# Neighbourhood attention on one core: the scores of the two new row tiles moved to the head of each step of TensorE's queue

## What is computed

```python
def one_row(r):
    rs = clip(r - 4, 0, rows - 8)
    k_blk, v_blk = the rows rs .. rs+7, the columns near each query
    s = einsum(q_row, k_blk); s = where(mask, s + bias, -1e30)
    p = softmax(s, axis=(-2, -1))
    return einsum(p, v_blk)
```

## Time and profile before

| | |
|---|---|
| time of the runs | 2304.22 us median of 3 (2302.72 to 2304.95) |
| time of the profiled execution | 2304.31 us |
| its span | 2302.5 us, 32169 instructions |
| TensorE products busy | 2245.8 us, 98% |
| VectorE busy | 1227.9 us, 53% |
| ScalarE busy | 902.1 us, 39% |
| GpSimd busy | 1074.2 us, 47% |
| chain that ended last | 87% of it TensorE |

### The profile page before, as it was taken

One profiled execution on the slowest core, in us unless ns is written; L12 is line 12 of the kernel. 1 busy time (PEld: TensorE's weight loads), 2 busy tenths in 40 slices (PEclk: granted clock), 3 DMA queues, 4 the chain that ended last, 5 costly groups with the idle time before them and its releaser, 6 DMA issues.

```text
span 2302.5 us, 32169 instructions
## 1 busy us (share of the span) xinstructions
PE 2245.8 (98%) x11948; PEld 1840.5 (80%) x11948; DVE 1227.9 (53%) x2065; ACT 902.1 (39%) x1793; POOL 1074.2 (47%) x777
## 2 busy tenths in 40 slices
PE   7999999999999999999999999999999999999998
PEld 6788888888788888888879867767878888888886
DVE  4644444546654444577753255555575444347767
ACT  5531111256223333344654345554642333334443
POOL 4112222467988888400234322313789888780000
PEclk9999999999999999999999999999999999999999
DMA  5121111342343323553353434243523433338334
GB/s 215 46 83 46 47 46 46 129 167 108 115 132 138 110 96 110 214 213 95 107 178 102 138 91 103 68 129 120 193 81 131 159 103 108 103 103 327 97 96 156
DMA packets 138573, 279.11 MB, mean 121 GB/s; under 512 B 34531, under 2 KB 55602, under 8 KB 136370
## 3 DMA queue, kind: packets, MB, share of 16 engines
q1 hardware_dynamic: 138418, 277.05, 36.2%
HBM read 207.80 MB, written 69.23 MB: 120 GB/s over the span
## 4 chain that ended last, share of the span: by engine, by line
PE 87%; DVE 3%; POOL 2%; ACT 1%; issue 1%; DMA 1%; SPq 0%; DVEq 0%; POOLq 0%; ACTq 0%
PE PS L2114 26%; PE PS L2116 26%; PE PS L2115 26%; PE PS L2396 2%; PE PS L2583 2%; PE PS L2601 2%; PE PS L2504 1%; POOL wlo L827 1%; DVE SB L1851 1%; PE PS L2429 1%; PE PS L2492 1%; PE PS L2384 1%; POOL rstd L856 0%; PE PS L2517 0%; PE PS L2516 0%
## 5 line engine op out<-in xcount | busy, mean ns | idle before, releaser
L2114 PE MATMUL PS<-AOP,OPS 128*128 128x512 f32 x1216 | 474.3, 390 | 5.1 <-DVE AOP L1666 3.2
L2116 PE MATMUL PS<-AOP,OPS 128*128 128x512 f32 x1216 | 473.5, 389 | 0.0
L2115 PE MATMUL PS<-AOP,OPS 128*128 128x512 f32 x1216 | 473.4, 389 | 0.0
L827 POOL TENSOR_TENSOR wlo<-stage,whi 128x1024 fp32r<-128x1024 f32 (+1 forms) x88 | 207.8, 2366 | 407.5 <-ACT whi L1057 407.2
L880 POOL TENSOR_TENSOR OPS<-TW,OPS 128x512 fp32r<-128x512 f32 x176 | 260.8, 1497 | 77.3 <-ACT OPS L1143 77.3
L2114 PE MATMUL PS<-aT,whi 128*128 128x512 f32 (+1 forms) x672 | 273.7, 407 | 7.3 <-DVE bdK L1917 3.6
L2114 PEld LDWEIGHTS PS<-AOP,OPS 128*128 128x128 f32 x1216 | 228.3, 188 | 54.4 <-POOL OPS L880 4.0
L2116 PEld LDWEIGHTS PS<-AOP,OPS 128*128 128x128 f32 x1216 | 228.3, 188 | 47.5
L2115 PEld LDWEIGHTS PS<-AOP,OPS 128*128 128x128 f32 x1216 | 228.4, 188 | 47.1
L2116 PE MATMUL PS<-aT,wlo 128*128 128x512 f32 (+1 forms) x672 | 261.4, 389 | 0.0
L2115 PE MATMUL PS<-aT,whi 128*128 128x512 f32 (+1 forms) x672 | 260.5, 388 | 0.0
(11 more groups left out here) (213 smaller groups left out, 4062.4 us busy)
## 6 DMA issues: line engine op xcount, KB each, us to landing
stage<-in_w SPq DMA_DIRECT2D x100, 512.0 KB, 3.8
hidden_scratch<-HT SPq DMA_DIRECT2D x154, 256.0 KB, 2.2
SRAW<-hidden_scratch SPq DMA_DIRECT2D x154, 256.0 KB, 2.6
stage<-in_wpack SPq DMA_DIRECT2D x76, 512.0 KB, 3.3
BW<-in_w SPq DMA_DIRECT2D x16, 1024.0 KB, 8.0
h_scratch<-Hb SPq DMA_DIRECT2D x24, 512.0 KB, 3.2
Hb<-h_scratch SPq DMA_DIRECT2D x24, 512.0 KB, 6.0
cat_scratch<-OC SPq DMA_DIRECT2D x14, 512.0 KB, 3.0
```

The source lines that it names most:

```text
L827: pool.tensor_tensor(wlo[:, slot, cols], stage[:, slot, cols], whi[:, slot, cols].bitcast(F32), ALU.subtract)\
L2114: pe.matmul(dst, stat[0], mov[0], start=start, stop=False, skip_group_check=onto)
L2115: pe.matmul(dst, stat[0], mov[1], start=False, stop=False, skip_group_check=onto)
L2116: return pe.matmul(dst, stat[1], mov[0], start=False, stop=stop, skip_group_check=onto)
```

## The change

`pair_scores(T)` moves from behind `filler(T)` to the head of the step, ahead of `turn_probs` of tile T-3 and of `filler(T)`. No instruction is added or taken away, and no wait is altered. The other engines' queues stay as they are.

```diff
             tiles = HP * ROWS
             for T in range(0, tiles + 4, 2):
+                if T < tiles:
+                    pair_scores(T)
                 if 0 <= T - 3 < tiles:
                     turn_probs(R_ROW + T - 3)
                 filler(T)
-                if T < tiles:
-                    pair_scores(T)
                 if 0 <= T - 4 < tiles:
                     pair_values(T - 4)
                 if 0 <= T - 2 < tiles:
                     turn_probs(R_ROW + T - 2)
                 filler(T + 1)
```

## The result

The changed kernel takes 2314.11 us (median of six runs, 2312.63 to 2315.2) against 2304.14 us for the kernel before beside it (six runs, 2302.72 to 2304.95): ratio 1.0043, 95% interval 1.0032 to 1.0053, so 10 us slower. The profiled execution took 2313.19 us with a span of 2311.4 us, 8.9 more than before.

The account below looks back on a forecast made before the run. TensorE's own time bounds the loop's first 200 us; in the last 53 us the chain through VectorE and ScalarE counts too. 5.6-1.2+0.7+2.4 = +7.5 us on 2304.31 gives 2311.8 us, range 2305.0 to 2316.0.

Parts of the forecast that it names:

- Joints in dense steps: TensorE, steps 4 to 76: changed neighbours among products cost 0.15 us per step in 37 steps, +5.6 us.
- S-Tr in the 360-column form: Start of the last score product to the following transposes of probabilities: taken as 0.77 us, as scores to values.
- F-V: Projection piece followed by value products: 0.33 us against 0.23 for projection to transposes, +0.10 per step.
- Tr-F: Transposes followed by projection: 0.30 us behind scores against 0.24 behind projection, +0.05 rounded per step.
- Waits in the dense part: First 200 us of the loop: four transpose waits go, -1.2 us; scores of four steps wait 0.2 each, +0.7.
- Waits in the tail: Last 53 us of the loop: new waits of scores and values +6.3 us, old waits that vanish -5.1.
- Waits that go: Last 53 us of the loop: old waits of transposes, projection and scores vanish, -5.1 us in sum.
- five small waits: Loop's tail: new waits at four score pairs (tiles 80, 86, 92, 94) and the values of tile 77, together 1.2 us.
- the clock plays no part: Both loop stages: TensorE's clock is at its full level, so nothing was booked for it.
- That the joints cost nothing: Rival, TensorE's joints: their 6.8 us vanish and +0.7 of waits is left, 2305.0 us; chance 0.14.
- That the head frees the chain: Rival, whole loop: earlier peaks, exponentials and normalising shrink TensorE's waits by 5.3 us, 2299.0 us; chance 0.04.
- That the head waits in every dense step: Rival, dense part: late peaks hold the scores in each of 38 steps, 11.4 us on top, 2323.2 us; chance 0.08.

Follow-up runs that it names:

- Run 3: Kernel before, old order, with the projection piece of steps 0 to 76 cut in two around the scores: 2309.83 us, ratio 1.0019.
- Run 5: Changed kernel run again: 2312.87 us, ratio 1.0040; then with ScalarE's last weight split in the loop behind tile 90, not 89: 2311.14 us, ratio 1.0032.
- runs 1: Kernel before with scores moved to the step's head only in steps 0 to 76, old order from step 78: 2309.59 us, ratio 1.0019.
- run 8: Changed kernel with VectorE's three operand splits one place later and ScalarE's two weight splits moved to tiles 80 and 92: 2307.08 us, ratio 1.0010.
- run 6: Changed kernel with VectorE's operand splits of tiles 82, 88 and 94 one place later, behind the next tile's peak: 2308.11 us, ratio 1.0017.

## Why the prediction held, and what it missed

The direction and the size held: +7.5 us forecast, +10 measured (2314.1 in a range of 2305.0 to 2316.0). Step by step:

- **Joints in dense steps, 37 x 0.15 = +5.6.** Right, and shown twice. From S(4) to S(78) the sum of the 37 steps went from 193.12 to 197.78 us. S-Tr in the 360-column form, the one price that no row of before had, is 0.77 as taken; F-V is 0.33, Tr-F 0.30. Run 3 produced the same kind of price with no wait at the head of the step. The Trainium skill (TensorEngine Tiling (Array Packing), Tiling Modes) says that a change of tiling mode drains TensorE; the trace agrees in the F-V row, 0.33 against the 0.23 of F-Tr. The 0.05 behind Tr, which that rule does not name, is in the trace too (0.30 against 0.25).
- **Waits in the dense part, -1.2+0.7 = -0.5.** The four waits of 0.3 at Tr went and four of 0.27 at S came, as forecast. But idle time between products is not the whole of a wait: the old steps with a wait were 0.53 us longer than their neighbours (5.66 against 5.13), the new ones 0.34 (5.61 against 5.27), since a product that does not wait starts before the one ahead of it has ended in the rows: F-Tr is 0.23 without a wait and 0.70 with it, of which the row counts 0.30 as idle (the product ahead is drawn 0.40 long), and Tr-F is 0.30 instead of 0.25. F-S is 0.33 without a wait and 0.67 with it. That gives 4 x (0.34-0.53) = -0.8, and another -0.3 came in the first two steps, where the new order has fewer joints. Measured +4.4 for the dense part; forecast 5.1.
- **Waits in the tail, +6.3-5.1.** The mechanism was right: S(84), S(88) and S(90) waited 2.25, 0.97 and 1.58 where 2.35, 1.0 and 1.7 were forecast, and Tr(78) and Tr(91) stopped waiting. **The step that failed stands in "Waits that go"**, where the held normalising of tile 91 was said to be "now behind S(94)" and booked as a gain. The same held normalising stands ahead of peak 93 in VectorE's queue, and S(94) waits for that peak: 1.70 us, where it was one of five small waits with 1.2 us together. (S(80), another of them, waited 0.95.) Run 5 took it away, and the loop gave back 1.8. A slip beside it: the list of splits names tile 80 where the one ahead of S(84) is that behind tile 82; the chain that was priced, and its 3.50 us, are the right ones. The tail measured +4.2 against +2.4.
- **What the sum left out.** I wrote that the clock plays no part, since it was at full level in the one profile that I had. The tail had an idle stretch of 2.3 us already, and its clock fell in one profile of three before. The new waits add idle time in the same place, and in the changed kernel's profiles the falls cost about 1.5, 3.0 and 4.5 us. How the 8.6 us at full clock become the 10 of the runs (9 by the ratio of run 5) stays open. In the mean of three profiles each, the loop is 11.1 longer, and the stretches around it 1.5 shorter, where falls come and go in both kernels. The longer wait for L827 behind the loop does not belong to the order: it is 1.1, 2.3 and 1.5 us in the kernel before and 1.9, 1.8 and 1.5 in the changed one.
- **The rivals.** That the joints cost nothing is refuted by the rows of runs 1 and 3. That the head frees the chain is refuted by the waits at S(84) and S(90), and by run 8: even with the tail's queues suited to it, the new order is 5.0 us behind the old one. That the head waits in every dense step did not happen: only the four steps with a held normalising do.

## What to carry to other kernels

When products are reordered in TensorE's queue, count the places where tiled and full-array products meet: here 0.10 us for each entry into a tiled product and 0.05 to 0.1 for the first full ones behind it, in every step, with no wait to show for it. Put a product that waits for another engine behind independent work, not ahead of it: at the head of a step nothing can run while it waits, and whatever stands ahead of its releaser in the other engine's queue (here an operand split and a normalising held by GpSimd) becomes TensorE's. When a wait is struck off because an instruction has moved, see who else stands behind the same late instruction; and cheap moves in the other queues, such as the one line of run 6, can be worth as much as a good part of a reordering: that line gave back 4.5 of the 8.6 us.

## What was unexpected

- VectorE's normalising of a tile in SBUF takes 0.4 us and 2.35 us when GpSimd's L827 has started 0.2 us ahead of it, while the peak, which reads scores in PSUM, took its usual 0.53 us wholly within an L827 (peak at 1428.36, L827 from 1427.11 to 1429.49, in the kernel before). A 2.4 us instruction on an engine at 47% set the waits of Tr(78) and Tr(91) in the old order and of S(94) in the new one, beside the four of the dense part in either; moving its trigger by one tile was worth 1.8 us.
- TensorE's clock fell in this loop in one of three profiled executions of the unchanged kernel, for 1.5 us of time, with no idle stretch longer than 2.3 us in the loop. One profile can show none, and the next one has it.
